# Hybrid streaming encoder step: queries and keys of a tile turned within the next, receptance ahead of values, frames ahead of the third weights

## What is computed

```
p = x @ w_in                                     # first 1792 columns: time mixing; the rest: attention
# attention half (2056 columns: q, k, v of 512, 8 forget gates, 512 output gates)
q, k, v, fl, og = split(p[:, 1792:])
logf = log_sigmoid(fl + b_f);  q = rms_norm(q) * q_g;  k = rms_norm(k) * k_g;  c = cumsum(logf)
# time mixing half
xs = pr + (prev - pr) * mu                       # prev: the frame before
xr, xk, xv, xw, xa, xg = split(xs)               # receptance, keys, values, low-rank inputs
decay = exp(-exp(w(xw)));  a = sigmoid(a0 + xa @ a2);  k = xk * (1 + (a - 1) * k_a);  kk = xk * k_k / norm
# per frame and head:  S = S * decay + (S @ -kk) (kk * a)^T + v k^T;   y = S @ r
...
m = concat(rwkv_out, fox_out) @ w_out;  h = layer_norm(ALPHA * x + m)
out = layer_norm(ALPHA * h + moe(h))             # top 2 of 32 experts: (silu(h w1) * (h w3)) @ w2
```

## Time and profile before

| | us |
|---|---|
| median of 3 runs (lowest to highest) | 3857.66 (3852.83 to 3857.68) |
| profiled execution, its own time | 3855.51 |
| its span, first instruction to last | 3853.7 |
| PE busy in it | 3629.9 (94%) |
| VectorE, ScalarE, GpSimd busy | 1628.0, 954.7, 236.8 |

### The profile page before, as it was taken

One profiled execution on the slowest core, in us unless ns is written; L12 is line 12 of the kernel. 1 busy time (PEld: TensorE's weight loads), 2 busy tenths in 40 slices (PEclk: granted clock), 3 DMA queues, 4 the chain that ended last, 5 costly groups with the idle time before them and its releaser, 6 DMA issues. The chain is left out here.

```text
span 3853.7 us, 77787 instructions
## 1 busy us (share of the span) xinstructions
PE 3629.9 (94%) x30285; PEld 2174.0 (56%) x30286; DVE 1628.0 (42%) x3569; ACT 954.7 (25%) x1730; POOL 236.8 (6%) x350
## 2 busy tenths in 40 slices
PE   7999997999999999988999989978999999999988
PEld 4444446888888888874555655543333333333333
DVE  1221224666666666666777645560111111111108
ACT  2222221323232323225555521110000000000003
POOL 0000001000000000001111000000000000000005
PEclk9999998999999999988999999988999999999999
DMA  5122212000000000002211152226566567744427
GB/s 218 61 74 74 74 59 61 10 10 19 10 19 10 19 11 19 11 9 81 59 56 56 45 189 92 99 83 269 216 265 255 198 267 283 299 152 159 158 113 305
DMA packets 145519, 430.34 MB, mean 112 GB/s; under 512 B 30696, under 2 KB 73840, under 8 KB 132976
## 3 DMA queue, kind: packets, MB, share of 16 engines
q1 hardware_dynamic: 126736, 359.27, 25.1%
q0 software_dynamic: 11616, 42.21, 3.1%
q10 hardware_dynamic: 6912, 25.17, 1.7%
HBM read 750.99 MB, written 78.27 MB: 215 GB/s over the span
## 5 line engine op out<-in xcount | busy, mean ns | idle before, releaser
L297 PE MATMUL fp<-f_w,f_xT 128*128 128x512 f32 (+1 forms) x1360 | 533.8, 547 | 9.8 <-DMA f_w<-in_w_in 9.5
L716 PE MATMUL rp_pa<-r_xT,w_rwkv 128*128 128x128 f32 x3808 | 483.7, 281 | 11.4 <-DMA r_xT<-scratch_xT 11.4
L716 PEld LDWEIGHTS rp_pa<-r_xT,w_rwkv 128*128 128x128 f32 x3808 | 449.8, 193 | 46.4 <-issue 35.2
L297 PEld LDWEIGHTS fp<-f_w,f_xT 128*128 128x128 f32 x1360 | 244.7, 200 | 262.7 <-issue 261.0
L2851 PE MATMUL e_H<-rows_in,e_xT 128*64 128x512 f32 x768 | 346.0, 604 | 19.7 <-DMA rows_in<-in_moe_w 18.0
L2852 PE MATMUL e_H<-fy,e_xT 128*64 x768 | 345.8, 604 | 0.0
L2870 PE MATMUL e_Y<-e_w,e_gT 128*64 128x512 f32 x768 | 339.8, 595 | 1.0 <-DMA e_w<-in_moe_w 1.0
L2852 PE MATMUL e_H<-e_w,e_xT 128*64 x768 | 339.8, 595 | 0.0
L2851 PE MATMUL e_H<-shared,e_xT 128*64 128x512 f32 x768 | 339.8, 595 | 0.0
L2871 PE MATMUL e_Y<-e_w,e_gT 128*64 x768 | 339.8, 595 | 0.0
L2851 PEld LDWEIGHTS e_H<-rows_in,e_xT 128*64 128x64 f32 x768 | 106.7, 140 | 238.7 <-issue 214.1
(11 more groups left out here) (434 smaller groups left out, 5601.5 us busy)
## 6 DMA issues: line engine op xcount, KB each, us to landing
e_w<-in_moe_w SPq DMA_DIRECT2D x144, 2048.0 KB
fy<-in_moe_w SPq DMA_DIRECT2D x48, 2048.0 KB
rows_in<-in_moe_w SPq DMA_DIRECT2D x48, 2048.0 KB
shared<-in_moe_w SPq DMA_DIRECT2D x48, 2048.0 KB
scratch_ypad<-e_y ACTq DMA_DIRECT2D x48, 512.0 KB, 2.9
scratch_xT<-f_xT SPq DMA_DIRECT2D x17, 512.0 KB
r_xT<-scratch_xT SPq DMA_DIRECT2D x17, 512.0 KB, 3.7
scratch_h<-m_h SPq DMA_DIRECT2D x17, 512.0 KB, 2.6
```

The costliest lines, as they stand in the source:

```text
L297: mm = eng.matmul(out, xT[:, slot, k, :], w[:, k, a:a + n], start=(k == 0), stop=(k == KD - 1))
L716: mm = eng.matmul(pre_bank(bank)[:, f * P:(f + 1) * P], w[:, d, (i + f) * P:(i + f + 1) * P], xT[:, slot, d, :], start=(d == 0), stop=(d = ...
```

## The change

It has five parts. The constants are made by GpSimd inside the block of the first projection, and SP loads frames of tile 0, weights q and k, frames of tile 1, weights v, the small vectors, weights fg. In the first projection (written out over the tiles, no loop any more) the turns qT and cT of tile t stand behind product k of tile t + 1 and kT behind its product v; f stands behind q (in tile 0 behind v), the running sums behind v; xT has a store and a semaphore of its own. In the time mixing the pieces r are projected, copied and shifted ahead of v; the three turns move behind `turned_products(t, 2)` and `products(t, 2)` of the next tile, `keyed_values` behind them; VectorE makes R before the new state, `masked` before "fin", and within it y and the shifted values between mrb and mk. SP waits for the first gather ahead of the third weights, and the second gather moves to the start of the experts' block.

```
 def constants(nc, ctx):
-    with nc.Block() as block:
-        @block.gpsimd
-        def _(pool):
+    def make(pool):
...
+    keep["make_constants"] = make
 def fox_projection(nc, io, keep):
-        W_PARTS = {"fg": (3 * DG, FCOLS), "q": (0, DG), "k": (DG, 2 * DG), "v": (2 * DG, 3 * DG)}
+        W_PARTS = {"q": (0, DG), "k": (DG, 2 * DG), "v": (2 * DG, 3 * DG), "fg": (3 * DG, FCOLS)}
...
+            frames(0)
+            weights("q")
+            weights("k")
+            frames(1)
+            weights("v")
...
+            weights("fg")
+            sp.dma_start(keep["w_rwkv"][:, :, :], w_rows[:, :, 0:RCOLS]).then_inc(keep["w_rwkv_loaded"], 16)
...
+            for t in range(TILES):
+                sp.wait_ge(*xpe.after("xT1", t))
+                if t + 2 < TILES:
+                    frames(t + 2)
+                sp.wait_ge(*xact.after("xT1", t))
+                sp.dma_start(io["xT"][t, :, :], xT[:, t % 2, :, :].rearrange("p k t -> p (k t)"))\
+                  .then_inc(turned_stored[t % 2], 16)
+                if t:
+                    stores(t - 1)
+            stores(NT)
...
         def _(pool):
-
+            keep["make_constants"](pool)
...
+            def gate_logits(t):
+                eng.wait_ge(w_loaded["fg"], 16)
+                eng.wait_ge(*dve.after("carry", t - 1))
+                product(t, 3 * DG, S[:, 0:HEADS]).then_inc(*gate_pe.done("f"))
...
+            def tile(t):
+                eng.wait_ge(*xact.after("xT1", t))
+                part(t, "q", 0, Q[:, :])
+                if t:
+                    gate_logits(t)
+                part(t, "k", DG, K[:, :])
+                if t:
+                    turn_queries(t - 1)
+                    turn_sums(t - 1)
+                if t < NT:
+                    turn_x(t + 1)
+                part(t, "v", 2 * DG, V[:, :])
+                if t:
+                    turn_keys(t - 1)
+                else:
+                    gate_logits(t)
+                gate_sums(t)
+                part(t, "g", 3 * DG + HEADS, G[:, :])
...
 def rwkv(nc, io, keep):
-                    ("zg", (2,), ("act", "g")), ("ss", (3,), ("act", "nrm")), ("v", (0,), ("act", "v")),
-                    ("r", (1,), ("act", "r")), ("vT", (2,), ("act", "vT")), ("bT", (0,), ("act", "bT")),
-                    ("kT", (1,), ("act", "kT")), ("ab", (2, 3), ("dve", "x1")), ("b", (0, 1), ("dve", "mrb")),
-                    ("kk", (2, 3), ("dve", "mk")), ("akv", (0, 1), ("act", "akv"))]
+                    ("zg", (2,), ("act", "g")), ("ss", (3,), ("act", "nrm")), ("r", (1,), ("act", "r")),
+                    ("v", (0,), ("act", "v")), ("ab", (2, 3), ("dve", "x1")), ("b", (0, 1), ("dve", "mrb")),
+                    ("kk", (2, 3), ("dve", "mk")), ("kT", (0,), ("act", "kT")), ("bT", (1,), ("act", "bT")), ("vT", (0,), ("act", "vT")), ("akv", (0, 1), ("act", "akv"))]
...
             def decays(u, s):
-                turn(u, "vT", 2, xs[:, 8:12, :], pdve.after("xv", u))
-                turn(u, "bT", 0, bt, pdve.after("B", u))
-                turn(u, "kT", 1, kt, pdve.after("K", u))
                 decay_ab(u, s)
...
                 turned_products(t, 2)
-                keyed_values(t)
+                if isinstance(t, int) and t == NT:
+                    eng.wait_ge(state_dve, 2)
+                turn(t, "kT", 0, kt, pdve.after("K", t))
+                turn(t, "bT", 1, bt, pdve.after("B", t))
                 if following:
                     project_x(u, s, j + slot)
                 products(t, 2)
+                turn(t, "vT", 0, xs[:, 8:12, :], pdve.after("xv", t))
                 if not first:
                     mean(t - 1, *pdve.after("mk", t))
+                keyed_values(t)
+                turned_products(t, 3)
                 fill("l", 0)
-                turned_products(t, 3)
                 fill("l", 1)
...
-            def masked(u):
+            def masked(u, t=None):
...
+                if t is not None:
+                    sum_of_y(t)
+                shift(u, "v", pre.after("vT", u - 1))
                 eng.wait_ge(*pre.after("kk", u))
...
                 if following:
                     normed_keys(u)
                     scaled_keys(u, s)
-                    values(u)
+                    shift(u, "r")
                     decayed(u, s)
+                    received(u, s)
                 new_state(t, 1)
+                if following:
+                    masked(u, t)
+                else:
+                    sum_of_y(t)
                 put(dve, "fin", t, eng.tensor_tensor(st[:, :, :], st[:, :, :], e1[:, slot, 1, :, C:C + 1].broadcast_to([P, PAIRS, C]),
                                                      ALU.mult))
...
 def mix(nc, io, keep):
             second_row(0, "w1")
+
+            sp.wait_ge(keep["e_x_loaded"][0], 16)
             first_row(0, 0, "w3")
             second_row(0, "w3")
...
-            for s in (0, 1):
-                gather_frames(eng, io, keep, s, keep["frame_of"][:, s:s + 1])
+            gather_frames(eng, io, keep, 0, keep["frame_of"][:, 0:1])
...
 def experts(nc, io, keep):
             pool.begin(eng)
+            gather_frames(eng, io, keep, 1, keep["frame_of"][:, 1:2])
```

More of the change, by code:

```diff
@@ L149, in constants, with step @@
-    keep["constants"] = n[0]
+    keep["constants"] = sum(1 if s[2] is None else 2 for s in shapes) + 7
+    def make(pool):
+        n = [0]
+        def step(ins):
+            n[0] += 1
+            ins.then_inc(ready, 1)
+            return n[0]
+        for out, back, op, col, row, base, fill in shapes:
+            count = step(pool.memset(out[:, :], back))
+            if op is not None:
+                pool.wait_ge(ready, count)
+                step(pool.affine_select(out=out[:, :], in_=out[:, :], compare_op=op, fill=fill, base=base,
+                                        pattern=[[col, P]], channel_multiplier=row))
+        step(pool.iota(ids[:, 0, :], pattern=[[1, EXPERTS]], base=0, channel_multiplier=0))
+        count = step(pool.iota(ids[:, 1, :], pattern=[[1, GROUPS], [0, PER_GROUP]], base=0, channel_multiplier=0))
+        pool.wait_ge(ready, count)
+        step(pool.tensor_copy(keep["expert_id"][:, :], ids[:, 0, :]))
+        step(pool.tensor_copy(keep["group_of"][:, :], ids[:, 1, :]))
+        count = step(pool.memset(halves[:, :], 0.0))
+        pool.wait_ge(ready, count)
+        step(pool.memset(halves[0:DH, 0:DH], 1.0))
+        step(pool.memset(halves[DH:P, DH:P], 1.0))
+        pool.wait_ge(ready, n[0])
+        assert n[0] == keep["constants"]
@@ new lines, in product, with part @@
+            def product(t, a, out):
+                for k in range(KD):
+                    mm = eng.matmul(out, xT[:, t % 2, k, :], w[:, k, a:a + out.shape[1]], start=(k == 0), stop=(k == KD - 1))
+                return mm
+            def part(t, name, a, out):
+                eng.wait_ge(w_loaded["fg" if name == "g" else name], 16)
+                eng.wait_ge(*act.after(name, t - 1))
+                product(t, a, out).then_inc(*pe.done(name))
+            def gate_logits(t):
+                eng.wait_ge(w_loaded["fg"], 16)
+                eng.wait_ge(*dve.after("carry", t - 1))
+                product(t, 3 * DG, S[:, 0:HEADS]).then_inc(*gate_pe.done("f"))
@@ L305, in tile, with gate_sums, turn_queries @@
+            def gate_sums(t):
+                eng.wait_ge(*dve.after("logf", t))
+                eng.wait_ge(*turned_dve.after("cT", t - 1))
+                eng.matmul(S[:, 8:16], keep["upto"][:, :], lf[:, t % 2, :], start=True, stop=True)
+                eng.matmul(S[:, 16:24], keep["ones"][:, :], lf[:, t % 2, :], start=True, stop=True)\
+                   .then_inc(*gate_pe.done("cum"))
+            def turn_queries(t):
                 eng.wait_ge(*dve.after("q2", t))
-                eng.wait_ge(*dve.after("kT", t - 1))
+                eng.wait_ge(*turned_dve.after("kT", t - 1))
@@ L322, in _ @@
+            turn_x(0)
+            for t in range(TILES):
+                tile(t)
+            turn_queries(NT)
+            turn_sums(NT)
+            turn_keys(NT)
         @block.scalar
@@ L813, in prepare @@
                 head_sums(u)
-                for name in "vr":
+                for name in "rv":
                     for f in range(4):
@@ L822, in turned_products @@
                 if n == 2:
-                    eng.wait_ge(*pdve.after("mrb", t))
+                    eng.wait_ge(*pdve.after("xT1", t))
                 else:
```

328 lines of the change are left out of this document (148 added, 180 removed).

## The result

The changed kernel takes 3763.74 us (median of 4 runs, 3759.89 to 3765.22) against 3855.24 before on the same chip: a ratio of 0.9761, 95% interval 0.9749 to 0.9773. The profiled execution is the fastest of the four (3759.89, span 3757.8), so the profile's difference, 95.9 in the span, is some 4 larger than that of the medians.

A forecast was written before the change was run, and what follows sets the result against it. PE, busy 94% of the span, was taken as the bound, time being won only from its waits or lower clock; 8.7 + 33 + 0.4 + 23.8 + 4.8 = 70.7 off 3855.5 gave 3785, with the median's 2.2 3787 us, range 3772 to 3811.

The forecast's parts named there:

- the supply of instructions: Time mixing boundaries: the denser stretch makes PE wait more for its own instructions, 5 us lost (bounds 0 and 24).
- the 0.62: First projection: PE's wait per tile for the copy of the turned queries goes, full-clock tile 32.41 - 0.62 = 31.8 us.
- the third product: Time mixing boundary: starts at 1101.42, 0.15 behind x1, ends at 1102.52; 3.48 instead of 5.26, 1.8 us saved per boundary.
- the clock drops of the projection: Tiles 1 to 16: no drop to 0.50 any more; with the removed wait -33 us (bounds -6 and -35).
- The start: First load out at 0.9 instead of 5.62, tile 0 ends at 46.6 instead of 55.29: -8.7 us (-6 to -11).
- The sum's 2.2 for the slow clock: Tile 0 of the first projection: 2.2 us for a slow clock at first, as q and k take 16.3 instead of 13.7.
- The experts' term: Mixture of experts: frames turned at about 2611.8 instead of 2616.6, -4.8 us (bounds -1 to -6), third weights hidden by 2.
- (a): Rival, first projection: clock still drops once per tile, a tile takes 33.5, term -6, 3814 us; chance 0.12.
- (d): Rival, first projection: three short groups per tile each cost a clock drop of 1.7, +49 instead of -33, 3869 us; chance 0.03.
- (b): Rival, time mixing: instruction supply eats the boundary gain, 1.5 per boundary given back, 3806 us; chance 0.11.
- (c): Rival, time mixing: the wait moves from r_ar to mk or the turned values, boundary gains nothing, 3810 us; chance 0.05.
- The forecast margin: Time mixing boundary: mk ends near 1106.5, PE comes to the sums that wait for it at 1107.0, covered by 0.5.

The follow-up runs named there:

- before64: The kernel before the change, with 32 turns of the identity (64 PE instructions, result unread) added ahead of the time mixing's first product; 3859.02 us.
- u_fox: The changed kernel with the constants in a block of their own and the first projection of the kernel before; 3813.08 us.
- u_moe: The changed kernel with both gathers back ahead of the experts' block and the third weights issued at once; 3767.56 us.
- own_block: The changed kernel with the constants back in a block of their own, the new order of loads kept; 3767.25 us.
- own_bank: The changed kernel with the time mixing's first group of decays written to the unused half of banks CA instead of PB; 3763.32 us.
- after64: The changed kernel with 32 turns of the identity (64 PE instructions, result unread) added ahead of the time mixing's first product; 3763.34 us.
- orders: The changed kernel with three other orders of the small products in the first projection, four tiles each (wait, long, both); 3789.13 us.
- orders2: As orders, with the wait kept at 0.7 and eight 8-column products added per tile, placed near or far from the turns; 3792.14 us.
- mean_between: The kernel before the change, with the mean of y moved between the keyed values and the second inverse product; 3858.16 us.
- the order "wait": Tiles 1 to 4 of orders, against the changed kernel: keys turned directly behind queries and sums, gates between q and k; 32.47 us per tile.
- one half alone: The changed kernel with the turns of kt and bt back ahead of the decays, the early receptance kept; 3789.00 us.
- turns_alone: The changed kernel with the turns left moved, but receptance, R, masks, y, fin and the values' shift in the order of before; 3833.05 us.

## Why the prediction was wrong

**The step that failed is the supply of instructions:** "The freed time makes this stretch denser ... I take 5 off (0.3 per boundary; bounds 0 and 24)". No gain lies within these bounds, though the sentence before names rows with 3.4 us of such waits in the kernel before, which a new order can give back. It gave back 4.5; against the forecast that is 9.5 of the 25.2 that are missing, the largest part. With this term right the sum would still have been near 3777, so the rest below counts too. What the runs show of these waits: PE stops where it comes to a border of code before the next piece is there, 2.3 to 2.9 behind the start of its packet, and where that is moves with the code (before64). In the new order two turns, the turn of the values and the mean stand among the 64-column products, and mk ends some 1.6 ahead of the keyed values. In tiles 1 to 14 the changed kernel and the seven others with its order of the time mixing (u_fox, u_moe, own_block, own_bank, after64, orders, orders2) have one stop, of 0.2 in tile 12 of own_block; so such stops are rare there, not impossible, and in tile 15 own_block has one of 1.5. Which part of the new order does most was not separated; in the old order a microsecond of longer products is enough (mean_between). The Trainium skill, "Runtime: NRT & Kernel Launch", section "Instruction fetch mechanics", has the crossing of a block mostly hidden; tiles 1 to 14 of the new order agree with it, the old order (up to 1.3 in the earlier trace rows) does not.

**Two sizes were short for one reason.** A wait was priced at the idle time in its row, and a product at its modelled end. In the projection the 0.62 was taken off as 0.62 and a tile forecast at 31.8; the order "wait", with a row of 0.71, costs 32.47 - 31.57 = 0.90. At the boundary the third product was taken to end 1.10 behind its start; the first inverse product follows after 0.89 (1039.73 to 1040.62). That is 3.6 and 3.4 in all. The mechanisms were those named: r_ar is no longer waited for, what remains is the wait for x1 (0.37), and the clock drops of the projection went with the order and come back with it (u_fox). The fall of the clock in the time mixing (1.1) was in no term.

**The start** came out at its size, with the first load at 1.05 (forecast 0.9) and the queries' product at 10.21 (11.3); own_block shows the mechanism. The sum's 2.2 for the slow clock should have been 2.6 by the two numbers beside it. **The experts' term** is 5.7 for 4.8, with the third weights hidden. **Stages outside the change** were 5.4 faster in this profile; the body of the experts alone varies by 5.7 from kernel to kernel, and the medians' difference (91.5) is smaller than the profiles' by 4.4. No run shows a cause for this part, and nothing in the change explains it.

**The rivals.** (a) and (d) fall with the granted clock of 1.00 over 480 us, (b) with the absence of waits for instructions in tiles 1 to 14, (c) with mk ready 1.6 ahead of its use. The forecast margin there was 0.5, because its sum left out the mean of y, which stands ahead of the keyed values and takes 1.0.

## What to carry to other kernels

A wait that a profile shows can also go away: bound a contended resource from both sides, starting from what it costs already. Price a wait by the distance between the starts of the instructions around it, with the wait and without, not by the idle time in its row alone. Before an early producer is credited with the wait that it removes, ask which work then stands in that place as cover for the next engine: here one half alone brought a third of the gain, and the other alone a loss.

## What was unexpected in the hardware

A wait of 3.1 in a stretch where PE is otherwise busy cost a fall of the grant to 0.50 behind it in every tile (turns_alone, 0.97 over 800 us), where waits of 1.70 and 0.63 in the same place cost none in most tiles. And moving code by 64 instructions, without any other change in the tiles, moves single tiles by up to 1.5 us (before64: tile 9 takes 63.70 instead of 65.18). A packet of instructions takes 0.9 to 1.6 us in the time mixing of the kernel before, but in the stops PE went on only 2.3 to 2.9 behind its start.
